# One more Strassen pair in the second block of each branch of the merge, and other blocks' forms of activations

## The chip, the core and the metric

The kernel runs on one core of a Trainium2 chip. The metric is the device time of one execution in microseconds (us); lower is better. A difference of less than 0.2% of it can't be told from no change.

## What is computed

One encoder layer on 256 tokens of width 2048, in float32. Two mixers, latent attention (`y_a`) and a matrix-memory recurrence (`y_b`), read the same normed input `u`; the merge weighs their projections with gates that are projections of `u` as well. The changed part is the merge:

```python
merged = jax.nn.sigmoid(gate_a) * (y_a @ p_a) + jax.nn.sigmoid(gate_b) * (y_b @ p_b)
x = x + merged @ w_out
```

`gate_a` and `gate_b` are columns of `u @ w_in`. Each of `p_a`, `p_b` and the two gates is a product of 256 x 2048 activations with 2048 x 2048 weights, in column blocks of 512. The cross attention and the conv-GLU feed-forward layer that follow are not touched.

## The kernel before

**Precision.** A float32 product is made of three products of rounded parts: every operand x is split into `x_hi` (rounded to fp32r) and `x_lo = x - x_hi`, and hi*hi, hi*lo and lo*hi are added up in PSUM (`three`, L641 to L643). ACT makes `w_hi` of the weights, DVE makes `w_lo`.

**The weight stream.** Weights come as chunks of 128 x 1024 (512 KB) through four slots of `w_raw`, `w_hi` and `w_lo`. The SP queue asks for the chunk of a slot anew once DVE has made `w_lo` from the old one (`lo_made`); ACT may write `w_hi` of a slot once PE is done with it (`w_used`). Two chunks are a *pair*, and there is room for two pairs: step n of the loops on ACT and DVE makes the weights of pair n + 2, while PE works on pairs n and n + 1.

**The merge** is 7 blocks (`MBLOCKS`) of 8 pairs (`KPB`): blocks 0 and 1 take `y_a` with `p_a`, 2 and 3 take `y_b` with `p_b`, 4 to 6 take `u` with the gates' weights. A block makes two column blocks of 512 for both halves of 128 tokens, in four banks of PSUM. A pair is two steps of 128 along the contraction. It is done in one of two ways:

- *plain* (`merge_plain`): 8 products of 128 x 512, each by `three`, so 24 matmuls.
- *fast* (`fast_pair`): the 2 x 2 blocks of a pair (two token halves, two column blocks) are multiplied by Strassen's scheme, with 7 products, so 21 matmuls. Four of them take sums of weights, `um_sum` (made by DVE in `fast_sums`, L1887 to L1892; split by ACT into `um_hi` at L1236 and by DVE into `um_lo` at L1907), and four take sums of activations, the pair's *form* (three of the products, e5, e6 and e7, take both). The products e1, e5, e6, e7 go into four extra banks, those of the block before. The last fast pair of a block is followed by `extra_sums`: ACT copies e1 out of PSUM (L1255), then DVE adds the others up in four steps (L1916 to L1922); `merge_main` (L1957) adds all to the block's own banks when the block is done.

`MFAST = (3, 6)` says which pairs of every block are fast: 14 in all. A form belongs to one pair of activations and is shared by the blocks that read the same activations, so there are 6 forms. `merge_form_sums` (DVE, five instructions, L1934 to L1942), `merge_form_high` (ACT, L1242) and `merge_form_low` (DVE, L1947) make one. `FORM_AT` says at which step (block, pair) of the loops the form of a given number is made.

**Order.** Each engine runs its program in the written order. On ACT, step n is: the copy of e1 where pair n is the block's last fast one, then `w_hi` of pair n + 2, then a form's high part, which waits until DVE has made the form's sums. On DVE: `extra_sums` for the last fast pair, `merge_main` for the block's last pair, then the weights of pair n + 2, then the form's sums. PE starts a block only when the extra sums of the block before are read (`extras_read`) and the first chunk's `w_lo` is made (`lo_made`).

Of the kernel before, what the change touches and what calls it, by code (L numbers as in the profile page):

```python
# [37 lines left out]
BLK = 512  # L38
# [15 lines left out]
MFAST = (3, 6)  # L54
MSUMS = MBLOCKS * len(MFAST)
MFORMS = 3 * len(MFAST)
G_GB = G_MERGE + MBLOCKS * 2 * KPB
G_WOUT = G_GB + KPB
FORM_AT = {(0, 2): 1, (1, 2): 2, (2, 2): 3, (3, 2): 4, (4, 2): 5}
# [58 lines left out]
def build(nc, x, x_t, mem, mem_by_feature, positions, cols_d, mats_d, stream, out):  # L118
    ctx = ExitStack()
    with ctx:  # L120
# [148 lines left out]
        def m_form(i):  # L269
            return (nm_hi[:, i, :], nm_sum[:, i, :], nm_lo[:, i, :]) if i < 4 else (  # L270
                nu_hi[:, i - 4, :], nu_sum[:, i - 4, :], nu_lo[:, i - 4, :])

        def m_fast(n):
            b, p = n // KPB, n % KPB
            return len(MFAST) * b + MFAST.index(p) if b < MBLOCKS and p in MFAST else None

# [112 lines left out]
        def _(pe):  # L389
# [303 lines left out]
            def merge_fast(b, p):  # L693

                i = len(MFAST) * (b // 2 if b < 4 else 2) + MFAST.index(p)
                hi, raw, lo = m_form(i)
                fast_pair(G_MERGE + 2 * (KPB * b + p), m_fast(KPB * b + p), i,
                          lambda k, rows: tuple(m_acts[b][:, 2 * p + k, half, rows] for half in range(2)),
                          lambda part: (hi[:, part], lo[:, part]), lambda m: (um_hi[:, m, :], um_lo[:, m, :]),
                          lambda c: m_bank(b, c), lambda c: m_bank(b + 1, c), p == MFAST[0], p == MFAST[-1])  # L700

            for b in range(MBLOCKS):
                for p in range(KPB):
                    if p == 0 and b:
                        pe.wait_ge(sem("extras_read"), 5 * b)
                    if p == 0 and b == 2:
                        pe.wait_ge(sem("yb_lo"), 4 * NBLK)
                    if p == 1 and b == MBLOCKS - 1:
                        pe.wait_ge(sem("mg_parts"), b)
                        merged_T(0)  # L710
                    if p == MFAST[0] and b:
                        pe.wait_ge(sem("mg_parts"), b)
                    if p == MFAST[0] and b == MBLOCKS - 1:
                        pe.wait_ge(sem("mg_lo"), 2)
                    if p in MFAST:
                        merge_fast(b, p)
                    else:
                        merge_plain(b, p)
# [187 lines left out]
        def _(act):  # L906
# [344 lines left out]
            for n in range(MBLOCKS * KPB):  # L1251
                b, p = n // KPB, n % KPB
                if p == MFAST[-1]:
                    act.wait_ge(sem("fast_done"), len(MFAST) * (b + 1))
                    act.activation(um_sum[:, 0, :], ps[:, m_bank(b + 1, 0), :], ACT.Copy).then_inc(sem("extras_read"), 1)  # L1255
                if m_fast(n + 2) is not None:
# [4 lines left out]
                if n == 0:  # L1261
                    merge_form_high(0)
# [213 lines left out]
        def _(dve):  # L1476
# [448 lines left out]
            def merge_form_sums(i):  # L1925

                q = MFAST[i % 2]
                act_t = (y_a, y_b, u)[i // 2]
# [3 lines left out]
                if i == 4:  # L1932
# [356 lines left out]
def lay_out(i):  # L2289
# [134 lines left out]
```

## Time and profile before

| | us |
|---|---|
| median of 3 runs | 1724.99 |
| lowest and highest | 1724.23, 1725.16 |
| the profiled execution's own time | 1725.04 |
| its span, from the first to the last instruction | 1723.3 |
| PE busy | 1717.2 |
| DVE busy | 1306.4 |
| ACT busy | 987.8 |

Matmuls overlap in the pipeline, so the time that one takes is longer than the distance from its start to the next one's start; what a stretch of matmuls costs is read from starts. Where a row of the timeline stands for several instructions (x2), its time runs from the first one's start to the last one's end. A time in brackets at a row's end is how long the engine stood idle ahead of it, and for whom. Block 0 of the merge begins at 488.14 us.

### The profile page before, as it was taken

To read this page: it belongs to the slowest core of one execution; us is meant where nothing else is said; L and a number is where in the kernel's file an instruction comes from. 1 tells how busy PE (TensorE), PEld (TensorE's weight loads), DVE (VectorE), ACT (ScalarE), POOL (GpSimd) and SP (SyncE) were. 2 spreads that over 40 slices of the span, in tenths; PEclk is the share of its full clock that TensorE was granted. 3 is DMA by queue.
4 is the path that set the end of the run, shared out by engine and by line. 5 is a ranking of instruction groups with operands and counts; after the bars stand their busy time and mean duration, and the time that the engine had idled before them with its cause. 6 is when DMAs were issued, how large, how long until landed. Compare 5 with 4: busy or idle time off the path is not lost.

```text
span 1723.3 us, 25512 instructions
## 1 busy us (share of the span) xinstructions
PE 1717.2 (100%) x8652; PEld 1459.6 (85%) x8652; DVE 1306.4 (76%) x1805; ACT 987.8 (57%) x1329; POOL 9.9 (1%) x22
## 2 busy tenths in 40 slices
PE   9999999999999999999999999999999999999999
PEld 7888888888888888888888888888888888888887
DVE  6788876667788888887665667777777777799888
ACT  7765655657854444555654565555555555566454
POOL 0000000000000000000000000000000000000000
PEclk9999999999999999999999999999999999999999
DMA  8566565554456666666755456555555555665565
GB/s 326 185 173 183 171 170 174 173 174 149 159 181 196 198 196 205 207 195 221 291 193 186 147 171 192 182 192 189 186 190 186 189 189 186 203 203 188 199 210 178
DMA packets 90970, 331.06 MB, mean 192 GB/s; under 512 B 10224, under 2 KB 10480, under 8 KB 89872
## 3 DMA queue, kind: packets, MB, share of 16 engines
q1 hardware_dynamic: 89424, 321.96, 56.8%
q0 software_dynamic: 1472, 8.12, 2.6%
q8 instruction: 46, 0.75, 0.2%
q14 instruction: 28, 0.23, 0.0%
HBM read 326.83 MB, written 2.10 MB: 191 GB/s over the span
## 4 chain that ended last, share of the span: by engine, by line
PE 99%; DMA 0%; DVE 0%; SPq 0%; ACT 0%; issue 0%
PE ps L424 22%; PE ps L427 11%; PE ps L643 10%; PE ps L642 10%; PE ps L641 10%; PE ps L405 8%; PE ps L407 8%; PE ps L406 8%; PE ps L527 1%; PE ps L528 1%; PE ps L526 1%; PE ps L571 1%; PE ps L570 1%; PE ps L740 0%; PE ps L585 0%; PE ps L578 0%
## 5 line engine op out<-in xcount | busy, mean ns | idle before, releaser
L1493 DVE TENSOR_TENSOR w_lo<-w_raw,w_hi 128x1024 fp32r<-128x1024 f32 x486 | 589.7, 1223 | 307.4 <-ACT w_hi L914 306.4
L914 ACT ACTIVATE w_hi<-w_raw 128x1024 fp32r<-128x1024 f32 x486 | 507.8, 1056 | 370.4 <-PE ps L427 150.0
L424 PE MATMUL ps<-u,w_hi 128*128 128x512 f32 x1664 | 580.8, 395 | 0.0
L427 PE MATMUL ps<-u,w_lo 128*128 128x256 f32 x1664 | 461.8, 278 | 0.0
L424 PEld LDWEIGHTS ps<-u,w_hi 128*128 128x128 f32 x1664 | 312.1, 188 | 72.1
L427 PEld LDWEIGHTS ps<-u,w_lo 128*128 128x128 f32 x1664 | 312.7, 188 | 0.2
L405 PE MATMUL ps<-w_hi,u 128*128 128x512 f32 x416 | 166.1, 399 | 1.0 <-DVE w_lo L1525 1.0
L407 PE MATMUL ps<-w_hi,u 128*128 128x512 f32 x416 | 162.4, 390 | 0.0
L406 PE MATMUL ps<-w_lo,u 128*128 128x512 f32 x416 | 162.2, 390 | 0.0
L643 PE MATMUL ps<-w_hi,h_lo 128*128 128x512 f32 x256 | 99.6, 389 | 0.0
L405 PEld LDWEIGHTS ps<-w_hi,u 128*128 128x128 f32 x416 | 78.3, 188 | 17.1 <-DVE u L1520 1.4
L407 PEld LDWEIGHTS ps<-w_hi,u 128*128 128x128 f32 x416 | 78.2, 188 | 16.8
L406 PEld LDWEIGHTS ps<-w_lo,u 128*128 128x128 f32 x416 | 78.4, 188 | 15.1
L1454 ACT ACTIVATE w_hi<-w_raw 128x1024 fp32r<-128x1024 f32 x52 | 54.6, 1054 | 30.9 <-PE ps L643 26.3
L2248 DVE TENSOR_TENSOR w_lo<-w_raw,w_hi 128x1024 fp32r<-128x1024 f32 x52 | 61.6, 1221 | 8.2 <-ACT w_hi L1454 8.2
L1231 ACT ACTIVATE w_hi<-w_raw 128x1024 fp32r<-128x1024 f32 x30 | 31.8, 1061 | 55.5 <-PE ps L643 39.6
L641 PE MATMUL ps<-w_hi,u 128*128 128x512 f32 x156 | 60.8, 390 | 0.0
L642 PE MATMUL ps<-w_lo,u 128*128 128x512 f32 x156 | 60.7, 389 | 0.0
L643 PE MATMUL ps<-w_hi,u 128*128 128x512 f32 x156 | 60.7, 389 | 0.0
L643 PEld LDWEIGHTS ps<-w_hi,h_lo 128*128 128x128 f32 x256 | 48.0, 188 | 9.9
L641 PE MATMUL ps<-w_hi,h_hi_b 128*128 128x512 f32 x138 | 53.7, 389 | 0.0
L642 PE MATMUL ps<-w_lo,h_hi_b 128*128 128x512 f32 x138 | 53.7, 389 | 0.0
(502 smaller groups left out, 2913.7 us busy)
## 6 DMA issues: line engine op xcount, KB each, us to landing
w_raw<-in_stream SPq DMA_DIRECT2D x600, 512.0 KB, 3.4
x_tok<-in_x SPq DMA_DIRECT2D x2, 1024.0 KB, 8.1
mem_raw<-in_mem_by_feature POOLq DMA_DIRECT2D x2, 1024.0 KB, 8.0
x_tok<-in_x POOLq DMA_DIRECT2D x2, 1024.0 KB, 8.9
mem_tok<-in_mem POOLq DMA_DIRECT2D x2, 1024.0 KB, 15.3
x_t<-in_x_t SPq DMA_DIRECT2D x7, 256.0 KB, 5.0
w_raw<-in_stream SPq DMA_DIRECT2D x4, 256.0 KB, 5.0
m_st<-ncm POOLq DMA_DIRECT2D x8, 128.0 KB, 6.4
```

The costliest lines, as they stand in the source:

```text
L405: pe.matmul(o, a_hi, b_hi, start=(kc == 0), stop=False)
L406: pe.matmul(o, a_hi, b_lo, start=False, stop=False)
L407: mm = pe.matmul(o, a_lo, b_hi, start=False, stop=(kc == last_kc))
L424: pe.matmul(ps[:, bank + m, :], w_hi[:, s, lo:lo + P], act[:, kc, :, :].rearrange("p h t -> p (h t)"), start=(kc == 0), stop=False)
L427: mm = pe.matmul(ps[:, bank + m, T:2 * T], w_lo[:, s, lo:lo + P], act[:, kc, 0, :], start=False, stop=(kc == KC - 1))
L641: pe.matmul(o, a_hi, b_hi, start=first, stop=False)
L642: pe.matmul(o, a_hi, b_lo, start=False, stop=False)
L643: return pe.matmul(o, a_lo, b_hi, start=False, stop=last)
L914: act.activation(w_hi[:, s, :], w_raw[:, s, :], ACT.Copy).then_inc(hi_made, 1)
L1454: act.activation(w_hi[:, s + k, :], w_raw[:, s + k, :], ACT.Copy).then_inc(hi_made, 1)
L1493: TTo(w_lo[:, s, :], w_raw[:, s, :], w_hi[:, s, :].bitcast(F32), ALU.subtract).then_inc(lo_made, 1)
L2248: TTo(w_lo[:, s + k, :], w_raw[:, s + k, :], w_hi[:, s + k, :].bitcast(F32), ALU.subtract).then_inc(lo_made, 1)
```

## The change

`MFORM` now lists for each block which pairs are fast and which form each takes. Blocks 0 and 2 have pairs 2 and 6 fast, blocks 1 and 3 pairs 2, 4 and 6, blocks 4 to 6 pairs 3 and 6 as before: 16 fast pairs in place of 14. There are 8 forms in place of 6, three for `y_a`, three for `y_b`, two for `u`. Forms 1, 2 and 3 are made in block 0 (steps 1, 2 and 5), forms 4, 5 and 6 in block 2 (steps 1, 2 and 5), form 7 in block 4; form 0 is begun ahead of block 0, as before, and is now finished ahead of the loop. Forms 3 and 6 are the first ones for the activations that follow, `y_b` and `u`. Before, the forms 1 to 5 were made in step 2 of blocks 0 to 4, one in each. On ACT its high part stands ahead of the weights of pair 2. The host's packing of the weights follows the new choice of pairs.

```diff
@@ -51,12 +51,14 @@
 G_ML = G_MLA + PAIRS * MLA_PER
 G_MERGE = G_ML + NBLK * KPB
 MBLOCKS = 7
-MFAST = (3, 6)
-MSUMS = MBLOCKS * len(MFAST)
-MFORMS = 3 * len(MFAST)
+MFORM = ({2: 0, 6: 1}, {2: 0, 4: 2, 6: 1}, {2: 3, 6: 4}, {2: 3, 4: 5, 6: 4}) + ({3: 6, 6: 7},) * 3
+MFAST = [sorted(forms) for forms in MFORM]
+MFIRST = [sum(len(at) for at in MFAST[:b]) for b in range(MBLOCKS + 1)]
+MSUMS = MFIRST[MBLOCKS]
+MFORMS = 8
 G_GB = G_MERGE + MBLOCKS * 2 * KPB
 G_WOUT = G_GB + KPB
-FORM_AT = {(0, 2): 1, (1, 2): 2, (2, 2): 3, (3, 2): 4, (4, 2): 5}
+FORM_AT = {(0, 1): 1, (0, 2): 2, (0, 5): 3, (2, 1): 4, (2, 2): 5, (2, 5): 6, (4, 2): 7}
 MG_BANK = (2, 0, 4, 0)
 G_CK = G_WOUT + (NBLK - 1) * KPB
 G_WOUTS = [G_WOUT, G_WOUT + KPB, G_WOUT + 2 * KPB, G_CK + KPB]
@@ -267,12 +269,12 @@
             return 4 * (c // 2) + 2 * (b % 2) + c % 2
 
         def m_form(i):
-            return (nm_hi[:, i, :], nm_sum[:, i, :], nm_lo[:, i, :]) if i < 4 else (
-                nu_hi[:, i - 4, :], nu_sum[:, i - 4, :], nu_lo[:, i - 4, :])
+            return (nm_hi[:, i % 4, :], nm_sum[:, i % 4, :], nm_lo[:, i % 4, :]) if i < 6 else (
+                nu_hi[:, i - 6, :], nu_sum[:, i - 6, :], nu_lo[:, i - 6, :])
 
         def m_fast(n):
             b, p = n // KPB, n % KPB
-            return len(MFAST) * b + MFAST.index(p) if b < MBLOCKS and p in MFAST else None
+            return MFIRST[b] + MFAST[b].index(p) if b < MBLOCKS and p in MFAST[b] else None
 
         def pair_slots(w, s):
             return w[:, s:s + 2, :].rearrange("p s n -> p (s n)")
@@ -692,12 +694,12 @@
 
             def merge_fast(b, p):
 
-                i = len(MFAST) * (b // 2 if b < 4 else 2) + MFAST.index(p)
+                i = MFORM[b][p]
                 hi, raw, lo = m_form(i)
                 fast_pair(G_MERGE + 2 * (KPB * b + p), m_fast(KPB * b + p), i,
                           lambda k, rows: tuple(m_acts[b][:, 2 * p + k, half, rows] for half in range(2)),
                           lambda part: (hi[:, part], lo[:, part]), lambda m: (um_hi[:, m, :], um_lo[:, m, :]),
-                          lambda c: m_bank(b, c), lambda c: m_bank(b + 1, c), p == MFAST[0], p == MFAST[-1])
+                          lambda c: m_bank(b, c), lambda c: m_bank(b + 1, c), p == MFAST[b][0], p == MFAST[b][-1])
 
             for b in range(MBLOCKS):
                 for p in range(KPB):
@@ -708,11 +710,11 @@
                     if p == 1 and b == MBLOCKS - 1:
                         pe.wait_ge(sem("mg_parts"), b)
                         merged_T(0)
-                    if p == MFAST[0] and b:
+                    if p == MFAST[b][0] and b:
                         pe.wait_ge(sem("mg_parts"), b)
-                    if p == MFAST[0] and b == MBLOCKS - 1:
+                    if p == MFAST[b][0] and b == MBLOCKS - 1:
                         pe.wait_ge(sem("mg_lo"), 2)
-                    if p in MFAST:
+                    if p in MFAST[b]:
                         merge_fast(b, p)
                     else:
                         merge_plain(b, p)
@@ -1250,16 +1252,16 @@
 
             for n in range(MBLOCKS * KPB):
                 b, p = n // KPB, n % KPB
-                if p == MFAST[-1]:
-                    act.wait_ge(sem("fast_done"), len(MFAST) * (b + 1))
+                if p == MFAST[b][-1]:
+                    act.wait_ge(sem("fast_done"), MFIRST[b + 1])
                     act.activation(um_sum[:, 0, :], ps[:, m_bank(b + 1, 0), :], ACT.Copy).then_inc(sem("extras_read"), 1)
+                if n == 0:
+                    merge_form_high(0)
                 if m_fast(n + 2) is not None:
                     fast_high(G_MERGE + 2 * (n + 2), m_fast(n + 2), um_sum, um_hi)
                 else:
                     split(Pos(G_MERGE), 2 * n)
                     split(Pos(G_MERGE), 2 * n + 1)
-                if n == 0:
-                    merge_form_high(0)
                 if (b, p) in FORM_AT:
                     merge_form_high(FORM_AT[b, p])
                 if b == MBLOCKS - 1 and p == 0:
@@ -1924,12 +1926,14 @@
 
             def merge_form_sums(i):
 
-                q = MFAST[i % 2]
-                act_t = (y_a, y_b, u)[i // 2]
+                b = (0, 0, 1, 2, 2, 3, 4, 4)[i]
+                act_t, q = m_acts[b], [p for p in MFAST[b] if MFORM[b][p] == i][0]
                 hi, dst, lo = m_form(i)
                 h1, h2 = n_raw[:, 0, :], n_raw[:, 1, :]
                 early, late = slice(0, P), slice(P, T)
-                if i == 4:
+                if i in (4, 5):
+                    dve.wait_ge(sem("fast_done"), MFIRST[2])
+                if i == 6:
                     dve.wait_ge(w_used, G_MERGE + 4 * KPB)
                 TTo(n_raw[:], act_t[:, 2 * q:2 * q + 2, 0, :].bitcast(F32), act_t[:, 2 * q:2 * q + 2, 1, :].bitcast(F32),
                     ALU.add).then_inc(sem("n_sums"), 1)
@@ -1975,28 +1979,27 @@
                         ).then_inc(sem("mg_lo"), 1)
 
             merge_form_sums(0)
+            merge_form_low(0)
             for n in range(MBLOCKS * KPB):
                 b, p = n // KPB, n % KPB
-                if p == MFAST[-1]:
+                if p == MFAST[b][-1]:
                     extra_sums(b, lambda c: m_bank(b + 1, c), um_sum)
                 if p == KPB - 1:
                     merge_main(b)
                 done = m_fast(n + 2)
                 if done is not None:
                     g = G_MERGE + 2 * (n + 2)
-                    if p + 2 == MFAST[0] and b:
+                    if p + 2 == MFAST[b][0] and b:
                         dve.wait_ge(sem("mg_parts"), b)
                     fast_sums(g, done, um_sum)
                     fast_lows(g, done, um_sum, um_hi, um_lo)
                 else:
                     split(Pos(G_MERGE), 2 * n)
                     split(Pos(G_MERGE), 2 * n + 1)
-                if n == 0:
-                    merge_form_low(0)
+                if (b, p - 1) in FORM_AT:
+                    merge_form_low(FORM_AT[b, p - 1])
                 if (b, p) in FORM_AT:
                     merge_form_sums(FORM_AT[b, p])
-                if (b, p - 1) in FORM_AT:
-                    merge_form_low(FORM_AT[b, p - 1])
                 if (b, p) == (1, 5):
                     dve.wait_ge(sem("sig_made"), TT * (NBLK + 1))
                     dve.wait_ge(sem("mg_parts"), 1)
@@ -2322,20 +2325,20 @@
         block(w_in, o0 + n * BLK)
     block(w_in, ga0)
     p_a, p_b, w_out = (np.asarray(i[n])[0] for n in ("p_a", "p_b", "w_out"))
-    def double(w, n0, v, m0):
+    def double(b, w, n0, v, m0):
 
         both = np.concatenate([w[:, n0:n0 + BLK], v[:, m0:m0 + BLK]], 1)
         for p in range(KPB):
             pair = both[2 * p * P:(2 * p + 2) * P].reshape(2, P, 1024).copy()
-            if p in MFAST:
+            if p in MFAST[b]:
                 pair[0] = np.roll(pair[0], BLK, axis=1)
             chunks.append(pair)
 
-    for w in (p_a, p_b):
-        for n in (0, 2):
-            double(w, n * BLK, w, (n + 1) * BLK)
+    for b in range(4):
+        w, n = (p_a, p_b)[b // 2], 2 * (b % 2)
+        double(b, w, n * BLK, w, (n + 1) * BLK)
     for n in range(3):
-        double(w_in, gb0 + n * BLK, w_in, ga0 + (n + 1) * BLK)
+        double(4 + n, w_in, gb0 + n * BLK, w_in, ga0 + (n + 1) * BLK)
     block(w_in, gb0 + 3 * BLK)
     for n in range(3):
         block(w_out, n * BLK)
```

DVE, block 0, from the weights of pair 4 on, which are made in step 2: `n_raw` is the raw sum of a form, `nm_sum` and `nm_lo` its sums and low part, `w_lo` the weights' low part, `um_sum<-w_raw` the first sum of weights of a fast pair (pair 6 in both). Before:

```order
L1493 TENSOR_TENSOR w_lo<-w_raw,w_hi 128x1024 x2
L1934 TENSOR_TENSOR n_raw<-y_a 128x512
L1937 TENSOR_TENSOR nm_sum<-n_raw 128x128
L1938 TENSOR_TENSOR nm_sum<-n_raw 128x128
L1940 SCALAR_TENSOR_TENSOR nm_sum<-nm_sum,n_raw 128x128
L1942 TENSOR_TENSOR nm_sum<-nm_sum,n_raw 128x128
L1493 TENSOR_TENSOR w_lo<-w_raw,w_hi 128x1024 x2
L1947 TENSOR_TENSOR nm_lo<-nm_sum,nm_hi 128x512
L1887 TENSOR_TENSOR um_sum<-w_raw 128x1024
```

The same place now, from the same weights (those of pair 4) on:

```order
L1495 TENSOR_TENSOR w_lo<-w_raw,w_hi 128x1024 x2
L1951 TENSOR_TENSOR nm_lo<-nm_sum,nm_hi 128x512
L1938 TENSOR_TENSOR n_raw<-y_a 128x512
L1941 TENSOR_TENSOR nm_sum<-n_raw 128x128
L1942 TENSOR_TENSOR nm_sum<-n_raw 128x128
L1944 SCALAR_TENSOR_TENSOR nm_sum<-nm_sum,n_raw 128x128
L1946 TENSOR_TENSOR nm_sum<-nm_sum,n_raw 128x128
L1495 TENSOR_TENSOR w_lo<-w_raw,w_hi 128x1024 x2
L1951 TENSOR_TENSOR nm_lo<-nm_sum,nm_hi 128x512
L1889 TENSOR_TENSOR um_sum<-w_raw 128x1024
```

Form 1's five sums have moved one step forward, behind the weights of pair 3; in their old place, between the weights of pair 4 and those of pair 5, stand the low part of form 1 and the sums of form 2, and one more low part stands ahead of pair 6's sums.

ACT, the end of block 0: `um_hi` is the high part of the weight sums of pair 6, the two rows behind it the weights of pair 7, and `um_sum<-ps` the copy of e1. Before:

```order
L1236 ACTIVATE um_hi<-um_sum 128x1024 [waits u_sums,fast_done]
L1236 ACTIVATE um_hi<-um_sum 128x1024 [waits u_sums]
L914 ACTIVATE w_hi<-w_raw 128x1024 [waits w_used,landed0]
L914 ACTIVATE w_hi<-w_raw 128x1024 [waits w_used,landed1]
L1255 ACTIVATE um_sum<-ps 128x512 [waits fast_done]
L914 ACTIVATE w_hi<-w_raw 128x1024 [waits w_used,landed2]
L914 ACTIVATE w_hi<-w_raw 128x1024 [waits w_used,landed3]
```

Now:

```order
L1238 ACTIVATE um_hi<-um_sum 128x1024 [waits u_sums,fast_done]
L1238 ACTIVATE um_hi<-um_sum 128x1024 [waits u_sums]
L916 ACTIVATE w_hi<-w_raw 128x1024 [waits w_used,landed0]
L916 ACTIVATE w_hi<-w_raw 128x1024 [waits w_used,landed1]
L1244 ACTIVATE nm_hi<-nm_sum 128x512 [waits n_sums]
L1257 ACTIVATE um_sum<-ps 128x512 [waits fast_done]
L916 ACTIVATE w_hi<-w_raw 128x1024 [waits w_used,landed2]
L916 ACTIVATE w_hi<-w_raw 128x1024 [waits w_used,landed3]
```

The high part of form 3, which waits for that form's sums (`n_sums`), stands in front of the copy of e1.

DVE, the end of block 0, from the low parts of pair 6's weight sums on: `um_sum<-ps` are the four extra sums. Before:

```order
L1907 TENSOR_TENSOR um_lo<-um_sum,um_hi 128x1024 x2
L1493 TENSOR_TENSOR w_lo<-w_raw,w_hi 128x1024 x2
L1916 TENSOR_TENSOR um_sum<-ps,um_sum 128x512
L1918 SCALAR_TENSOR_TENSOR um_sum<-ps,um_sum 128x512
L1920 TENSOR_TENSOR um_sum<-ps,um_sum 128x512
L1922 SCALAR_TENSOR_TENSOR um_sum<-ps,um_sum 128x512
L1493 TENSOR_TENSOR w_lo<-w_raw,w_hi 128x1024 x2
L1957 TENSOR_TENSOR pa<-ps,um_sum 128x1024 x2
```

Now:

```order
L1909 TENSOR_TENSOR um_lo<-um_sum,um_hi 128x1024 x2
L1495 TENSOR_TENSOR w_lo<-w_raw,w_hi 128x1024 x2
L1938 TENSOR_TENSOR n_raw<-y_b 128x512
L1941 TENSOR_TENSOR nm_sum<-n_raw 128x128
L1942 TENSOR_TENSOR nm_sum<-n_raw 128x128
L1944 SCALAR_TENSOR_TENSOR nm_sum<-nm_sum,n_raw 128x128
L1946 TENSOR_TENSOR nm_sum<-nm_sum,n_raw 128x128
L1918 TENSOR_TENSOR um_sum<-ps,um_sum 128x512
L1920 SCALAR_TENSOR_TENSOR um_sum<-ps,um_sum 128x512
L1922 TENSOR_TENSOR um_sum<-ps,um_sum 128x512
L1924 SCALAR_TENSOR_TENSOR um_sum<-ps,um_sum 128x512
L1495 TENSOR_TENSOR w_lo<-w_raw,w_hi 128x1024 x2
```

The sums of form 3 stand behind the weights of pair 7 and in front of the extra sums; block 2 has the same rows at its end, with form 6.

## Rows read from the trace of the kernel before

**Rows 1.** The page: busy time by engine; granted clock by slice.
```profile
PE 1717.2 (100%) x8652; PEld 1459.6 (85%) x8652; DVE 1306.4 (76%) x1805; ACT 987.8 (57%) x1329; POOL 9.9 (1%) x22
...
PEclk9999999999999999999999999999999999999999
```

**Rows 2.** Chain of waits, engine PE: line, releaser, total us, times, longest.
```profile
PE ps L439 <- DVE y_a L1513: 1.5, 1, 1.5
PE ps L405 <- DVE w_lo L1525: 1.0, 1, 1.0
```

**Rows 3.** Timeline of PE, merge: start us, us, engine, line, operation.
```profile
488.14 0.48 PE L641 MATMUL ps<-w_hi,y_a 128*128 128x512 f32 x1
...
499.13 0.39 PE L641 MATMUL ps<-w_hi,y_a 128*128 128x512 f32 x1
...
504.57 0.39 PE L641 MATMUL ps<-w_hi,y_a 128*128 128x512 f32 x1
...
509.40 0.39 PE L641 MATMUL ps<-w_hi,y_a 128*128 128x512 f32 x1
...
530.59 0.39 PE L641 MATMUL ps<-w_hi,y_a 128*128 128x512 f32 x1
...
572.92 0.39 PE L641 MATMUL ps<-w_hi,y_b 128*128 128x512 f32 x1
```

**Rows 4.** Timeline of DVE, block 0 of the merge.
```profile
491.41 0.68 DVE L1934 TENSOR_TENSOR n_raw<-y_a 128x512 f32<-128x512 f32 x1
...
492.99 0.29 DVE L1942 TENSOR_TENSOR nm_sum<-nm_sum,n_raw 128x128 f32<-128x128 f32 x1
...
510.58 2.36 DVE L1493 TENSOR_TENSOR w_lo<-w_raw,w_hi 128x1024 fp32r<-128x1024 f32 x2 [1.65 <-ACT w_hi L914]
512.86 0.69 DVE L1947 TENSOR_TENSOR nm_lo<-nm_sum,nm_hi 128x512 fp32r<-128x512 f32 x1
513.46 1.22 DVE L1887 TENSOR_TENSOR um_sum<-w_raw 128x1024 f32<-128x1024 f32 x1
...
520.18 1.22 DVE L1493 TENSOR_TENSOR w_lo<-w_raw,w_hi 128x1024 fp32r<-128x1024 f32 x1
...
525.96 0.69 DVE L1916 TENSOR_TENSOR um_sum<-ps,um_sum 128x512 f32<-128x512 f32 x1 [3.08 <-ACT um_sum L1255]
...
528.86 2.36 DVE L1493 TENSOR_TENSOR w_lo<-w_raw,w_hi 128x1024 fp32r<-128x1024 f32 x2
```

**Rows 5.** Timeline of ACT, block 0 of the merge.
```profile
491.44 1.27 ACT L1159 ACTIVATE sig<-ps,tiny 128x512 f32<-128x512 f32 x2
...
508.97 0.63 ACT L1242 ACTIVATE nm_hi<-nm_sum 128x512 fp32r<-128x512 f32 x1 [3.07 <-DVE nm_sum L1942]
509.50 1.99 ACT L914 ACTIVATE w_hi<-w_raw 128x1024 fp32r<-128x1024 f32 x2
...
525.33 0.60 ACT L1255 ACTIVATE um_sum<-ps 128x512 f32<-128x512 f32 x1 [3.71 <-PE ps L643]
```

**Rows 6.** Timeline of DVE, start of block 2.
```profile
571.27 2.36 DVE L1493 TENSOR_TENSOR w_lo<-w_raw,w_hi 128x1024 fp32r<-128x1024 f32 x2
...
575.81 3.49 DVE L1493 TENSOR_TENSOR w_lo<-w_raw,w_hi 128x1024 fp32r<-128x1024 f32 x3
...
582.76 1.23 DVE L1887 TENSOR_TENSOR um_sum<-w_raw 128x1024 f32<-128x1024 f32 x1 [1.82 <-DMA w_raw<-in_stream]
```

**Rows 7.** Tile w_raw, 488 to 660 us: issue to landing.
```profile
DMA to landing us min/median/max: 3.1/4.2/5.4
```

**Rows 8.** Timelines of PE and DVE, start of the program.
```profile
1.47 4.63 PE L439 MATMUL ps<-y_a 128*128 128x512 f32 x10 [1.47 <-DVE y_a L1513]
...
6.72 0.40 PE L407 MATMUL ps<-w_hi,u 128*128 128x512 f32 x1
...
8.83 0.47 PE L405 MATMUL ps<-w_hi,u 128*128 128x512 f32 x1 [1.02 <-DVE w_lo L1525]
...
7.99 0.69 DVE L1525 TENSOR_TENSOR w_lo<-w_raw,w_hi 128x512 fp32r<-128x512 f32 x1
```

## The prediction

> **What bounds the kernel now.** I read the page first: PE is busy for 1717.2 us of a span of 1723.3 us, and its granted clock is at full speed in every slice [rows 1]. So only two things can move the time: fewer matmuls, or PE standing idle. Second, PE's own waits: two, both in the program's first 9 us, 2.5 us in all [rows 2, 8]. In the merge PE never waits. The reader should see in it that a microsecond saved on ACT or DVE is worth nothing, and that one added there is free only as long as each chunk is ready when PE comes for it. The busy totals (DVE 1306.4 us) don't tell how near that is; the timelines do.
>
> **What a fast pair saves.** Pair 2 of block 0 is plain and runs from 499.13 to 504.57 us, 5.44 us for 24 matmuls. Pair 3 is fast and runs from 504.57 to 509.40, 4.83 us for 21 [rows 3]. A pair made fast gives 0.61 us; two give 1.22 us, 0.07% of the time. That is all that the change can win: the loads, the stores and everything behind the merge stay as they are.
>
> **What it adds.** Two fast pairs on ACT and DVE, and two forms, all in blocks 0 to 3, and new places for the rest. A fast pair takes DVE from 513.46 to 520.18, 6.72 us, against 2.28 us for a plain pair's two `w_lo` (510.58 to 512.86) [rows 4]. A form takes 1.87 us for its five sums (491.41 to 492.99, and the last one's 0.29) and 0.60 us for its low part (512.86 to 513.46). Behind the sums there is a third cost that no busy time shows. ACT, whose next job is the form's high part, stands still until the sums are done (3.07 us at 508.97), makes the high part (0.53 us, to 509.50), and only then the `w_hi` for which DVE's next step waits: DVE stands idle for 1.65 us at 510.58 [rows 4, 5]. So a form costs DVE 1.87 + 1.65 + 0.60 = 4.12 us where both engines are in step like this.
>
> **Block 0, by DVE's clock.** Block 0 keeps two fast pairs, so PE's work in it is unchanged: from 488.14 to 530.59 us [rows 3]. DVE's work grows from one form to three (the last for block 2), and the first fast pair moves from 3 to 2.
> - Form 0's sums end at 492.99 + 0.29 = 493.28. ACT is free (its sigmoids end at 491.44 + 1.27 = 492.71 [rows 5]) and makes the high part, 0.63 us; DVE's low part of 0.60 us ends at about 494.6. There pair 2's sums of weights begin.
> - Then, in the program's new order: pair 2 (fast) 6.72; weights of pair 3 2.28; form 1's sums 1.87 and the wait 1.65; pair 4 2.28; low part 0.60; form 2's sums 1.87 and the wait 1.65; pair 5 2.28; low part 0.60; pair 6 (fast) 6.72; pair 7 2.28; form 3's sums 1.87. That is 32.67 us, so 527.3.
> - The copy of e1 stands on ACT behind form 3's high part, which waits for these sums: 0.05 for the handing over, 0.53 for the high part, 0.63 from the start of the copy to DVE's first extra sum (525.33 to 525.96 [rows 4, 5]). Then four extra sums, 2.90 (525.96 to 528.86), and block 1's first `w_lo`, 1.22: 5.33 us. It is done at 532.6.
>
> Before, that `w_lo` was done at 528.86 + 1.22 = 530.08, just in time for PE's 530.59. PE restarts about 0.15 us after a `w_lo` that it waited for (7.99 + 0.69 = 8.68, matmul at 8.83 [rows 8]): at 532.75. PE stands idle for **2.2 us** at the start of block 1. On the way PE may wait some tenths for pair 5's or pair 6's weights. That adds nothing, since the chain at the block's end is DVE's.
>
> The trap here is DVE's idle 3.08 us ahead of the extra sums [rows 4]: form 3's sums (1.87 us) look as if they fit in. They don't, since that gap has been used up by two more forms at 4.12 us each, less what the earlier start gives back; what matters is when DVE gets there.
>
> **Block 2** has the same order with forms 4, 5 and 6, so the same 38.0 us from pair 2's first sum to the next block's first `w_lo`. Only its start differs. There DVE waits for a landing: the second chunk of block 2's pair 3 was asked for when `w_lo` of the chunk before it in its slot was done, about 575.81 + 2.36 = 578.2, and DVE began at 582.76, 4.6 us later [rows 6]; the loads of that stretch take 3.1 to 5.4 us [rows 7]. Pair 2's second chunk is asked for at 571.27 + 2.36 = 573.63, 0.7 us after the block's start at 572.92; so its sums begin 0.7 + 4.6 = 5.3 us after the start (DVE itself is free at 5.2), where in block 0 they begin 6.5 us after it. 5.3 + 38.0 + 0.15 = 43.4, against 42.33 us of PE's work in the block (530.59 to 572.92 is such a block [rows 3]): idle **1.1 us** at the start of block 3.
>
> **Blocks 1 and 3** have three fast pairs and no form's sums. DVE: 3 x 6.72 + 3 x 2.28 = 27.0 us from some 6 us after the start, so it is done at 33, and PE ends pair 6 at 42.33 - 0.61 - 5.44 = 36.3. The narrow place is pair 4, whose sums may begin only when PE is done with pair 2. DVE's part for a fast pair, 6.72 us, ends with two `um_lo` that are as large as two `w_lo` (2.28), so the pair's own `w_lo` are done some 4.4 us after PE's end of pair 2 and everything after 6.8; PE comes for the first after pair 3, 5.44 us, and for the first `um_lo` nine matmuls later, 5.44 + 9 x 0.227 = 7.5 us (0.227 is 5.44 over 24). Nothing waits. Blocks 4 to 6 keep their pairs; form 7 takes form 5's place.
>
> **Sum.** -1.22 + 2.2 + 1.1 = +2.1 us. Made against the profiled execution, 1725.04 us for a span of 1723.3, this gives a span of 1725.4; that execution is 0.05 us from the median, so 1724.99 + 2.1 = **1727.1 us**. The measurement tells no change within 0.2%, 3.4 us: I forecast no measurable difference, a little to the slow side.
>
> **Rivals.**
> - *The forms are hidden* (chance 0.08). DVE is idle 3.08 us before the extra sums of each block, and 417 us of the span in all. If the three forms of a block fit into such gaps, only the saving is left: 1724.99 - 1.22 = 1723.8. Against it speaks the count above; it would take a block 0 in which DVE reaches the extra sums 2 us sooner than I add up.
> - *PE's clock falls in the pause* (0.07), the one that ends on the other side. PE would meet a pause of 2.2 us in a dense stretch, and the trace of before has none above 1.5 us. At the program's start matmuls come every 0.44 us (ten in 4.63, the last one's end counted) where 0.227 is the rule, from 1.47 to 6.72 us [rows 8]; the page's clock row doesn't show it. If a pause brought this back for as long, 5.25 us at half speed would lose some 2.5 us: 1729.6, slower by 0.27%. One such fall decides it, as 1.3 us more than my sum does. Against it: behind the pause of 1.0 us at 8.83 matmuls go on at full speed. [...]
> - *The weights land late* (0.05). Block 2's chain starts at a landing. With 5.4 us in place of 4.6 it is 0.8 us later, and in blocks 1 and 3 the raw chunks come near to ruling too, some 0.5 us each: 1728.9. To pass 0.2% it would take landings 1.4 us later than 4.6, beyond all in [rows 7]; DMA has no bytes added, so I give it little.
> - *The stalls are there, of another size* is my forecast itself (0.80). Its bounds: block 3's pause gone (landings at 3.1 leave 1.0, so only if DVE is quicker than its rows) and block 1's at 1.5 give +0.3; both larger by half give +3.7. So 1725.3 to 1728.7.
>
> **Numbers.** Of the forecast's 0.80 some 0.03 lies above 0.2%; the clock adds 0.07, late landings 0.02: slower 0.12. Faster by 0.2% would need 3.4 us where 1.22 are to be had: 0.01. The rest, 0.87, is no change. The range leaves out the hidden forms below and the fallen clock above: 1725.3 to 1729.0.
>
> **What would show it.** PE has 6 matmuls fewer, 8646. In the chain of waits for PE there are two new rows that name `w_lo`, or the extra sums, of about 2.2 and 1.1 us, at the first matmul of blocks 1 and 3, and small ones inside blocks 0 and 2. On ACT the copy of e1 in blocks 0 and 2 is released by DVE's form sums and no longer by PE. In blocks 1 and 3, 0.61 us less between starts. Wrong would be: no wait of PE above 0.5 us in the merge (then DVE's steps are shorter or overlap), or matmuls at 0.44 us behind a pause.

## The result

The changed kernel takes 1727.49 us (median of 23 runs) against 1725.03 us for the kernel before (23 runs): ratio 1.0015, 95% interval 1.0009 to 1.0021. It is 2.5 us slower, inside the 0.2% that I had called no change. One execution of each kernel in that job was far slower (2134.86 us at a mean granted clock of 0.753, the one that was profiled, and 2888.43 us), and so was one of E1 below (1740.27 us at 0.948), and where falls of the clock are counted these three are left out. The rows shown here are those of E1, a second job of the same kernel: 1727.55 us, span 1725.8 us, clock 1.0.

The page of the changed kernel, engines' busy time and granted clock:

```profile
PE 1716.6 (99%) x8646; PEld 1458.5 (85%) x8646; DVE 1318.8 (76%) x1827; ACT 993.0 (58%) x1335; POOL 9.9 (1%) x22
...
PEclk9999999999999999999999999999999999999999
```

PE has 6 matmuls fewer and is busy 0.6 us less than in [rows 1], in a span that is 2.5 us longer. Its waits:

```profile
PE ps L643 <- DVE w_lo L1495: 3.0, 2, 1.8
PE ps L441 <- DVE y_a L1515: 1.5, 1, 1.5
PE ps L407 <- DVE w_lo L1527: 1.2, 1, 1.2
```

The last two are the start of the program, as in [rows 2]. The first is new: two waits for `w_lo` (L1495 is the old L1493), 3.0 us together, the longest 1.8. The timeline of PE shows where; the list of waits counts idle time from a matmul's modelled end, so I read the cost from starts:

```profile
488.17 0.48 PE L643 MATMUL ps<-w_hi,y_a 128*128 128x512 f32 x1
...
530.50 0.39 PE L645 MATMUL ps<-w_hi,y_a 128*128 128x512 f32 x1
532.70 0.47 PE L643 MATMUL ps<-w_hi,y_a 128*128 128x512 f32 x1 [1.80 <-DVE w_lo L1495]
533.00 0.39 PE L644 MATMUL ps<-w_lo,y_a 128*128 128x512 f32 x1
...
574.56 0.39 PE L643 MATMUL ps<-w_hi,y_b 128*128 128x512 f32 x1
...
616.66 0.39 PE L645 MATMUL ps<-w_hi,y_b 128*128 128x512 f32 x1
618.21 0.47 PE L643 MATMUL ps<-w_hi,y_b 128*128 128x512 f32 x1 [1.16 <-DVE w_lo L1495]
...
660.05 0.39 PE L643 MATMUL ps<-w_hi,u 128*128 128x512 f32 x1
```

One plain matmul follows the other after 0.227 us. Here there are 2.20 us between the last one of block 0 (530.50) and the first of block 1 (532.70), and 1.55 us between those of blocks 2 and 3 (616.66, 618.21). The kernel before reached the end of block 3 at 657.59 on its timeline:

```profile
657.59 0.39 PE L641 MATMUL ps<-w_hi,u 128*128 128x512 f32 x1
```

| from first matmul to first matmul | before, us | now, us | difference |
|---|---|---|---|
| block 0, with the pause behind it | 42.45 | 44.53 | +2.08 |
| block 1 | 42.33 | 41.86 | -0.47 |
| block 2, with the pause behind it | 42.33 | 43.65 | +1.32 |
| block 3 | 42.34 | 41.84 | -0.50 |
| all four | 169.45 | 171.88 | +2.43 |

(Before: 488.14, 530.59 and 572.92 in [rows 3] and 657.59 above; blocks 2 and 3 together took 84.67, halved here.) Behind a pause the second matmul comes 0.30 us after the first (532.70, 533.00), so blocks 1 and 3 each carry 0.07 us that is the restart's; a fast pair gave 0.54 to 0.57 us. The rest of the program is as long as it was.

DVE in block 0, in the order in which the prediction added it up:

```profile
494.00 0.69 DVE L1951 TENSOR_TENSOR nm_lo<-nm_sum,nm_hi 128x512 fp32r<-128x512 f32 x1 [0.70 <-ACT nm_hi L1244]
494.61 1.22 DVE L1889 TENSOR_TENSOR um_sum<-w_raw 128x1024 f32<-128x1024 f32 x1
...
503.60 0.68 DVE L1938 TENSOR_TENSOR n_raw<-y_a 128x512 f32<-128x512 f32 x1
...
507.12 2.36 DVE L1495 TENSOR_TENSOR w_lo<-w_raw,w_hi 128x1024 fp32r<-128x1024 f32 x2 [1.65 <-ACT w_hi L916]
...
510.00 0.68 DVE L1938 TENSOR_TENSOR n_raw<-y_a 128x512 f32<-128x512 f32 x1
...
513.51 2.36 DVE L1495 TENSOR_TENSOR w_lo<-w_raw,w_hi 128x1024 fp32r<-128x1024 f32 x2 [1.65 <-ACT w_hi L916]
...
523.11 2.35 DVE L1495 TENSOR_TENSOR w_lo<-w_raw,w_hi 128x1024 fp32r<-128x1024 f32 x2
525.38 0.68 DVE L1938 TENSOR_TENSOR n_raw<-y_b 128x512 f32<-128x512 f32 x1
...
528.43 0.69 DVE L1918 TENSOR_TENSOR um_sum<-ps,um_sum 128x512 f32<-128x512 f32 x1 [1.18 <-ACT um_sum L1257]
...
531.33 2.36 DVE L1495 TENSOR_TENSOR w_lo<-w_raw,w_hi 128x1024 fp32r<-128x1024 f32 x2
```

Pair 2's sums begin at 494.61 (I had 494.6). Form sums begin at 503.60, 510.00 and 525.38, and behind the first two DVE stands idle for 1.65 us, as it did once in [rows 4]. Where the kernel before came to the extra sums at 522.9 and waited 3.08 us for the copy of e1, DVE now comes at 527.25 and is then held for another 1.18 us. The last row is block 1's first `w_lo`, done at 531.33 + 1.22 = 532.55; PE's matmul is at 532.70. ACT in the same stretch:

```profile
505.50 0.63 ACT L1244 ACTIVATE nm_hi<-nm_sum 128x512 fp32r<-128x512 f32 x1 [5.02 <-DVE nm_sum L1946]
...
511.90 0.63 ACT L1244 ACTIVATE nm_hi<-nm_sum 128x512 fp32r<-128x512 f32 x1 [3.87 <-DVE nm_sum L1946]
...
527.28 0.63 ACT L1244 ACTIVATE nm_hi<-nm_sum 128x512 fp32r<-128x512 f32 x1 [5.22 <-DVE nm_sum L1946]
527.81 0.58 ACT L1257 ACTIVATE um_sum<-ps 128x512 f32<-128x512 f32 x1
```

ACT stands idle ahead of each of the three high parts, for DVE's sums, and the copy of e1 (L1257) starts at 527.81 right behind the third. PE was done with the last fast pair at about 525.4 (in the kernel before, where the copy waits for nothing else, it began at 525.33 [rows 5], in a block that started 0.03 us earlier). So the copy is late by 2.4 us for the sake of a form that is first used in block 2.

### The profile page after: what moved, and what is told of

It reads as the page before. It is cut to its first block, busy times and chain, and to the rows that moved or that the text cites. A ratio compares the mean times of both kernels' runs of the same rounds, so it can differ in the third digit from the quotient of the medians.

```text
span 2133.0 us, 25534 instructions
## 1 busy us (share of the span) xinstructions
PE 2127.2 (100%) x8646; PEld 1600.3 (75%) x8646; DVE 1332.3 (62%) x1827; ACT 1001.4 (47%) x1335; POOL 9.9 (0%) x22
## 4 chain that ended last, share of the span: by engine, by line
PE 99%; DMA 0%; DVE 0%; SPq 0%; ACT 0%; issue 0%
PE ps L426 22%; PE ps L429 11%; PE ps L644 10%; PE ps L643 10%; PE ps L645 10%; PE ps L409 9%; PE ps L407 9%; PE ps L408 8%; PE ps L528 2%; PE ps L529 1%; PE ps L530 1%; PE ps L572 1%; PE ps L573 1%; PE ps L587 0%; PE ps L742 0%; PE ps L580 0%
## 5 line engine op out<-in xcount | busy, mean ns | idle before, releaser
L1495 DVE TENSOR_TENSOR w_lo<-w_raw,w_hi 128x1024 fp32r<-128x1024 f32 x482 | 587.9, 1224 | 584.2 <-ACT w_hi L916 583.2
L426 PE MATMUL ps<-u,w_hi 128*128 128x512 f32 x1664 | 711.3, 456 | 0.0
L429 PE MATMUL ps<-u,w_lo 128*128 128x256 f32 x1664 | 526.2, 316 | 0.0
L426 PEld LDWEIGHTS ps<-u,w_hi 128*128 128x128 f32 x1664 | 329.9, 198 | 130.5
L429 PEld LDWEIGHTS ps<-u,w_lo 128*128 128x128 f32 x1664 | 338.5, 203 | 0.5
L407 PE MATMUL ps<-w_hi,u 128*128 128x512 f32 x416 | 194.8, 468 | 0.7 <-DVE w_lo L1527 0.7
L409 PE MATMUL ps<-w_hi,u 128*128 128x512 f32 x416 | 189.6, 456 | 0.0
L408 PE MATMUL ps<-w_lo,u 128*128 128x512 f32 x416 | 189.4, 455 | 0.0
L645 PE MATMUL ps<-w_hi,h_lo 128*128 128x512 f32 x256 | 116.6, 455 | 0.0
L409 PEld LDWEIGHTS ps<-w_hi,u 128*128 128x128 f32 x416 | 83.0, 200 | 35.1
L407 PEld LDWEIGHTS ps<-w_hi,u 128*128 128x128 f32 x416 | 82.4, 198 | 34.2 <-DVE u L1522 1.2
L644 PE MATMUL ps<-w_lo,u 128*128 128x512 f32 x156 | 71.4, 458 | 0.0
L645 PE MATMUL ps<-w_hi,u 128*128 128x512 f32 x156 | 71.2, 457 | 0.0
L643 PE MATMUL ps<-w_hi,u 128*128 128x512 f32 x156 | 71.1, 456 | 0.0
L644 PE MATMUL ps<-w_lo,h_hi_b 128*128 128x512 f32 x138 | 63.2, 458 | 0.0
L643 PE MATMUL ps<-w_hi,h_hi_b 128*128 128x512 f32 x138 | 62.9, 456 | 0.0
```

Of the source, the lines that this page charges most:

```text
L407: pe.matmul(o, a_hi, b_hi, start=(kc == 0), stop=False)
L408: pe.matmul(o, a_hi, b_lo, start=False, stop=False)
L409: mm = pe.matmul(o, a_lo, b_hi, start=False, stop=(kc == last_kc))
L426: pe.matmul(ps[:, bank + m, :], w_hi[:, s, lo:lo + P], act[:, kc, :, :].rearrange("p h t -> p (h t)"), start=(kc == 0), stop=False)
L429: mm = pe.matmul(ps[:, bank + m, T:2 * T], w_lo[:, s, lo:lo + P], act[:, kc, 0, :], start=False, stop=(kc == KC - 1))
L643: pe.matmul(o, a_hi, b_hi, start=first, stop=False)
```

## The experiments

All ran beside the kernel before, whose medians were 1724.99 (E1 to E4) and 1725.08 us (E5 to E8).

**E1, the changed kernel once more**, without an edit.

> The changed kernel as it is, for a profile at full clock. My theory (ACT and DVE fall behind in blocks 0 and 2 by the forms, and the copy of e1 stands behind the last form's high part): PE waits once at the first matmul of block 1, 2.2 us, and once at that of block 3, 1.1 us; blocks 1 and 3 are 0.61 us shorter; time 1727.1 us. Rival (the third fast pair is what starves PE): waits inside blocks 1 and 3, none above 0.5 us at their start. Rival (the clock falls in the pause): matmuls 0.44 us apart behind the first pause, granted clock under 1.000 in that stretch, and a time near 1729.

1727.55 us, ratio 1.0023 (1.0009 to 1.0036). The pauses are those above, 2.08 and 1.32 us, both at a block's start; inside blocks 1 and 3 no two starts are more than 0.31 us apart. This speaks against the third pair as the cause. The profiled execution kept its clock. But of 10 executions three had a mean granted clock of 0.999 and took 1728.86 to 1729.27 us, while seven at 1.000 took 1726.86 to 1727.66. In the first job it was 5 of 22, at 1728.47 to 1729.12.

**E2, the copy of e1 ahead of the high part.**

```diff
@@ on ACT, step n
                 if p == MFAST[b][-1]:
...
+                if p == 6 and (b, 5) in FORM_AT:
+                    merge_form_high(FORM_AT[b, 5])
...
-                if (b, p) in FORM_AT:
+                if (b, p) in FORM_AT and p != 5:
                     merge_form_high(FORM_AT[b, p])
```

> On ACT the high parts of forms 3 and 6 are made behind the copy of e1 and no longer ahead of it; all else is the changed kernel. Theory: the copy is no longer in the chain, so 0.05 + 0.53 + 0.63 = 1.2 us go from each pause: block 1's is 1.0 us, block 3's is gone; time 1724.9 us. Rival (only ACT's order matters, DVE's backlog doesn't): both pauses gone, 1723.8 us. Rival (the order on ACT doesn't matter): no change, 1727.1 us.

1724.91 us, ratio 0.9999 (0.9990 to 1.0008), as the theory said to 0.1 us. That closeness is in part luck: the pauses took 2.6 us less (1.27 and 1.32), not 2.3, from a time that was 0.4 us above the forecast. DVE at the end of block 0, then PE:

```profile
525.61 0.68 DVE L1940 TENSOR_TENSOR n_raw<-y_b 128x512 f32<-128x512 f32 x1
...
527.40 0.68 DVE L1920 TENSOR_TENSOR um_sum<-ps,um_sum 128x512 f32<-128x512 f32 x1
...
530.29 2.36 DVE L1497 TENSOR_TENSOR w_lo<-w_raw,w_hi 128x1024 fp32r<-128x1024 f32 x2
```

```profile
531.66 0.47 PE L643 MATMUL ps<-w_hi,y_a 128*128 128x512 f32 x1 [0.54 <-DVE w_lo L1497]
```

The extra sums follow form 3's sums without a wait. Block 0 with its pause takes 43.26 us (488.40 to 531.66), 0.8 us more than before and 1.27 less than in E1; block 3's pause is gone. So with DVE as late as it is, ACT's order was worth some 1.3 us of each pause, and DVE's lateness alone the other 0.8 of block 0's.

**E3, forms 3 and 6 in the next block.**

```diff
-FORM_AT = {(0, 1): 1, (0, 2): 2, (0, 5): 3, (2, 1): 4, (2, 2): 5, (2, 5): 6, (4, 2): 7}
+FORM_AT = {(0, 1): 1, (0, 2): 2, (1, 3): 3, (2, 1): 4, (2, 2): 5, (3, 3): 6, (4, 2): 7}
```

> Forms 3 and 6 (the first of the following activations) are made in step 3 of blocks 1 and 3 in place of step 5 of blocks 0 and 2. Theory: DVE reaches block 0's extra sums at 525.4, before the copy of e1 is there (525.96), as in the kernel before; no pause at the start of blocks 1 and 3, and blocks 1 and 3 have room for a form. Only the saving of 1.22 us is left: 1723.8 us. Rival (the forms 1, 2, 4, 5 alone already delay DVE past the extra sums): a pause of 0.5 us or more stays, 1724.5 us or above.

1724.14 us, ratio 0.9995 (0.9986 to 1.0004). No pause behind blocks 0 and 2, as expected, but 0.3 us too much. The place is the end of block 1, where DVE also weighs a block by a gate (the first row):

```profile
566.85 1.21 DVE L2006 TENSOR_TENSOR pa<-pa,sig 128x1024 f32<-128x1024 f32 x1
568.10 0.69 DVE L1918 TENSOR_TENSOR um_sum<-ps,um_sum 128x512 f32<-128x512 f32 x1
```

It comes to the extra sums at 568.10, while ACT's copy was there at 567.55; block 1's last matmul and block 2's first are 0.39 us apart, 0.16 us more than the usual 0.227. A form's sums cost nothing only where the engine has idle time left before the next point at which another engine waits for it.

**E4, the forms without the pairs.**

```diff
-MFORM = ({2: 0, 6: 1}, {2: 0, 4: 2, 6: 1}, {2: 3, 6: 4}, {2: 3, 4: 5, 6: 4}) + ({3: 6, 6: 7},) * 3
+MFORM = ({2: 0, 6: 1}, {2: 0, 6: 1}, {2: 3, 6: 4}, {2: 3, 6: 4}) + ({3: 6, 6: 7},) * 3
...
-                act_t, q = m_acts[b], [p for p in MFAST[b] if MFORM[b][p] == i][0]
+                act_t, q = m_acts[b], ([p for p in MFAST[b] if MFORM[b][p] == i] + [4])[0]
```

The second edit makes the two unused forms from pair 4, as before.

> All forms are made when and where the changed kernel makes them, but blocks 1 and 3 have two fast pairs (2 and 6); forms 2 and 5 are made and not used. Theory: both pauses stay as they are (2.2 and 1.1 us) and the saving is gone: 1725.0 + 3.3 = 1728.3 us. Rival (the third pair makes the pauses): no pause, 1725.0 us.

1728.61 us, ratio 1.0023 (1.0014 to 1.0033). The starts across the two pauses are 2.23 and 1.47 us apart, where E1 has 2.20 and 1.55. The pauses come with the forms alone; the third pairs take 1.1 us off (1728.61 to 1727.55). Four of 10 executions had a clock of 0.999, at 1729.82 to 1730.62 us.

**E5, one form less.** The kernel before's number of pairs and forms, at the changed kernel's places.

```diff
-MFORM = ({2: 0, 6: 1}, {2: 0, 4: 2, 6: 1}, {2: 3, 6: 4}, {2: 3, 4: 5, 6: 4}) + ({3: 6, 6: 7},) * 3
+MFORM = ({2: 0, 6: 1},) * 2 + ({2: 2, 6: 3},) * 2 + ({3: 4, 6: 5},) * 3
-FORM_AT = {(0, 1): 1, (0, 2): 2, (0, 5): 3, (2, 1): 4, (2, 2): 5, (2, 5): 6, (4, 2): 7}
+FORM_AT = {(0, 1): 1, (0, 5): 2, (2, 1): 3, (2, 5): 4, (4, 2): 5}
```

The number of forms, their numbering and the waits that go by it follow.

> Two fast pairs (2 and 6) in blocks 0 to 3 and two forms for each branch; the first form of the following activations stays in step 5 of blocks 0 and 2, ahead of the copy of e1 on ACT as in the changed kernel. Theory (the pauses come from DVE's backlog, to which each form in steps 1 and 2 adds 4.1 us): with one form less DVE makes the last form's sums by 523.2 in block 0, before the last fast pair is done, so nothing holds the copy; no pause, 1725.0 us. Rival (a form whose high part stands ahead of the copy makes a pause wherever it is): 1.2 us or more at the starts of blocks 1 and 3, 1727 us.

1725.09 us against 1725.08, ratio 1.0000 (0.9991 to 1.0009). No pause, with the high part still ahead of the copy. DVE in block 0, then ACT:

```profile
513.83 1.22 DVE L1889 TENSOR_TENSOR um_sum<-w_raw 128x1024 f32<-128x1024 f32 x1 [1.62 <-issue]
...
522.83 0.68 DVE L1936 TENSOR_TENSOR n_raw<-y_b 128x512 f32<-128x512 f32 x1
...
525.88 0.69 DVE L1918 TENSOR_TENSOR um_sum<-ps,um_sum 128x512 f32<-128x512 f32 x1 [1.18 <-ACT um_sum L1257]
```

```profile
524.73 0.63 ACT L1244 ACTIVATE nm_hi<-nm_sum 128x512 fp32r<-128x512 f32 x1 [3.21 <-DVE nm_sum L1944]
525.26 0.58 ACT L1257 ACTIVATE um_sum<-ps 128x512 f32<-128x512 f32 x1
```

The high part is out of the way at 525.26. The copy starts there, 37.22 us after the block's first matmul (488.04), against 37.19 in the kernel before (525.33 and 488.14), and the extra sums start at 525.88, as early as before. The order on ACT does harm only once DVE is late; both are needed for the full pause. But the copy is on time with nothing to spare. The form's sums end at 525.88 - 1.18 = 524.70, 1.5 us later than I expected: DVE stood idle for 1.62 us ahead of pair 6's sums (513.83). The profile names no releaser there, but pair 6's second chunk was asked for when pair 4's `w_lo` were done, at 509.51, and took 4.2 us to land. So one form less gave DVE 2.55 us (527.25 to 524.70), not 4.1; the rest it spent waiting for weights.

**E6, a longer pause.**

```diff
+                for _ in range(3 if i == 3 else 0):
+                    step(TTo(n_raw[:], act_t[:, 2 * q:2 * q + 2, 0, :].bitcast(F32),
+                             act_t[:, 2 * q:2 * q + 2, 1, :].bitcast(F32), ALU.add))
                 TTo(n_raw[:], ...
```

> The first sum of form 3 in block 0 is made four times over, some 0.72 us each, so 2.2 us are added to DVE's chain; all else is the changed kernel. Theory: the pause at the start of block 1 grows by the same 2.2 us to 4.2 us, and the time to 1727.5 + 2.2 = 1729.7 us. The clock: in some executions of the kernels with a pause of 2 us the mean granted clock was 0.999 and the time some 1.6 us longer; if the pause brings that about, it happens more often here, or always (1731.3 us), and the row of the stretch behind the pause shows a granted clock under 1 and matmuls about 0.44 us apart. Rival (the clock's dips have nothing to do with the pause): as often as in the changed kernel.

1731.39 us, ratio 1.0037 (1.0023 to 1.0051). The starts across the first pause are 4.37 us apart, 2.17 more than in E1. All five executions had a clock under 1 (0.999 or 0.998). Here a profile caught it. PE behind the pause, and the windows (the third number from the right is the granted clock):

```profile
535.21 0.47 PE L643 MATMUL ps<-w_hi,y_a 128*128 128x512 f32 x1 [3.98 <-DVE w_lo L1495]
535.51 0.40 PE L644 MATMUL ps<-w_lo,y_a 128*128 128x512 f32 x1
535.74 0.43 PE L645 MATMUL ps<-w_hi,y_a 128*128 128x512 f32 x1
535.98 0.63 PE L643 MATMUL ps<-w_hi,y_a 128*128 128x512 f32 x1
536.40 0.63 PE L644 MATMUL ps<-w_lo,y_a 128*128 128x512 f32 x1
...
538.96 0.59 PE L644 MATMUL ps<-w_lo,y_a 128*128 128x512 f32 x1
539.38 0.40 PE L645 MATMUL ps<-w_hi,y_a 128*128 128x512 f32 x1
```

```profile
488.00:530.00 42.00, 42.00 (x189) 34.48 (x188) 36.58 (x54) 22.16 (x28) 0.00 (x0) 1.00 0.59 188
530.00:535.00 5.00, 1.22 (x6) 0.68 (x4) 3.93 (x6) 4.68 (x6) 0.00 (x0) 1.00 0.00 0
535.00:539.00 4.00, 3.79 (x11) 3.05 (x12) 4.00 (x6) 0.00 (x0) 0.00 (x0) 0.62 0.63 178
539.00:543.00 4.00, 4.00 (x18) 3.30 (x17) 3.97 (x5) 1.02 (x2) 0.00 (x0) 0.95 0.61 216
```

Three matmuls still follow at 0.23 to 0.30 us, then eight are 0.42 to 0.43 us apart (535.98 to 539.38), then the old pace returns. 512 columns in 0.425 us are 1.2 GHz, in 0.227 us the 2.4 GHz level; the granted clock is 0.62 in the window from 535 to 539 and 0.95 in the next, into which the last 0.4 us fall, and it is 1.00 ahead of them, the pause itself included. Eight times 0.425 - 0.227 is 1.6 us, near to the 1.7 and 1.8 us that the executions at 0.999 took longer than those at 1.000 in E1 and E4 (medians). So it is likely that the same fall, behind one of the pauses, is what some executions of the changed kernel have; none of them was profiled. With a pause twice as long it came in all five.

"TensorE: Matmul & The Clock Gate" of the Trainium skill, section "Why this matters for your kernels", says that an idle gap of more than a certain length between bursts of matmuls sends PE back to half clock. The pause here, 3.98 us idle, is longer than that, and this trace agrees, with 1.6 us for one fall. The pauses of some 2 us in E1 and E4 are shorter than that, and yet the mean clock was 0.999 in 3 of 10 and 4 of 10 executions; there the measurement decides.

**E7, high parts one step later.**

```diff
-                if (b, p) in FORM_AT:
-                    merge_form_high(FORM_AT[b, p])
+                if (b, p - 1) in FORM_AT:
+                    merge_form_high(FORM_AT[b, p - 1])
```

> Forms in the steps of the changed kernel, but ACT makes each high part one step later, behind the next step's weights (and behind the copy of e1). Theory: DVE's wait of 1.65 us for w_hi behind each form's sums is gone (two in block 0, two in block 2) and the copy isn't held; DVE is at the extra sums by 524, before the copy; no pause at the starts of blocks 1 and 3: 1723.8 us. Rival (the amount of form work in the blocks is the cause): at least block 1's pause stays, 1 us or more, 1725 us.

1723.91 us, ratio 0.9993 (0.9984 to 1.0002). No pause; the four blocks take 168.26 us (487.81 to 656.07), 1.19 less than before. DVE in block 0:

```profile
504.81 0.29 DVE L1946 TENSOR_TENSOR nm_sum<-nm_sum,n_raw 128x128 f32<-128x128 f32 x1
505.02 2.35 DVE L1495 TENSOR_TENSOR w_lo<-w_raw,w_hi 128x1024 fp32r<-128x1024 f32 x2
...
509.47 0.29 DVE L1946 TENSOR_TENSOR nm_sum<-nm_sum,n_raw 128x128 f32<-128x128 f32 x1
509.68 2.35 DVE L1495 TENSOR_TENSOR w_lo<-w_raw,w_hi 128x1024 fp32r<-128x1024 f32 x2
...
525.63 0.69 DVE L1918 TENSOR_TENSOR um_sum<-ps,um_sum 128x512 f32<-128x512 f32 x1 [1.30 <-ACT um_sum L1257]
```

Behind both forms' sums the next `w_lo` follows at once, for ACT has made its `w_hi` while DVE was summing. The same number of forms in the same steps costs PE nothing when ACT isn't made to wait for them first. This edit does two things at once, it takes away DVE's waits and it puts the copy of e1 ahead of form 3's high part; E2 has the second alone and keeps 0.8 us of block 0's pause, so the first is worth at least that.

**E8, forms 3 and 6 in step 1 of blocks 1 and 3.**

```diff
-FORM_AT = {(0, 1): 1, (0, 2): 2, (0, 5): 3, (2, 1): 4, (2, 2): 5, (2, 5): 6, (4, 2): 7}
+FORM_AT = {(0, 1): 1, (0, 2): 2, (1, 1): 3, (2, 1): 4, (2, 2): 5, (3, 1): 6, (4, 2): 7}
```

> Forms 3 and 6 in step 1 of blocks 1 and 3, where DVE stands idle for 1.8 us until PE is done with the first fast pair; in the run that made them in step 3 DVE came 0.55 us late to block 1's extra sums and PE lost 0.2 us at the start of block 2. Theory: no pause at all, 0.2 us better than that run: 1723.9 us. Rival (step 1 delays the weight sums of pair 4, which PE then waits for): waits inside blocks 1 and 3, 1724.3 us or more.

1724.00 us, ratio 0.9994 (0.9985 to 1.0003), and no pause. DVE in block 1:

```profile
544.85 0.69 DVE L1938 TENSOR_TENSOR n_raw<-y_b 128x512 f32<-128x512 f32 x1
...
546.63 1.22 DVE L1889 TENSOR_TENSOR um_sum<-w_raw 128x1024 f32<-128x1024 f32 x1
```

The form's sums fill the time in which DVE had to wait for the first fast pair (1.82 us in E3), and pair 4's sums follow them without a gap. E3's small loss is gone (168.37 us for the four blocks, 168.66 in E3). E7 and E8 are both some 1.1 us better than the kernel before. The interval of each comparison takes in 1, so it rests on the starts: 168.26 us for the four blocks in E7 and 168.37 in E8, against 169.45. All 22 times of E7 and E8 (1723.34 to 1724.56) also lie below all 27 of the kernel before (1724.65 and more). Which of the two is better is not shown.

## Why the prediction was right

The time (1727.1 forecast, 1727.5 measured), the sign and the cause came out as forecast. The terms add up to +2.4 us measured (-0.97, +2.08, +1.32) where I had +2.1. They are off by +0.25, -0.12 and +0.22 us, so the sum is not right by large errors that cancel. By the terms of the sum:

- **Two fast pairs, -1.22 us.** -0.47 and -0.50 in blocks 1 and 3, -1.1 without the two restarts, and -1.08 to -1.19 in E8 and E7. Right in size, some 0.1 us too much; the restart behind a pause, 0.07 us each, I had left out.
- **The chain of DVE in block 0, a pause of 2.2 us.** 2.08. The start of pair 2's sums (494.6), of form 3's (525.4) and the end of block 1's first `w_lo` (532.6 forecast, 532.55 measured) were met to 0.1 us. E2, E5 and E7 take away one link each and give what the sum gives without it: 1724.9, 1725.0 and 1723.8 us forecast, 1724.91, 1725.09 and 1723.91 measured (in E2 in part by luck, and in E5 with 1.5 us of the margin that I expected gone, as said there).
- **The same chain in block 2, a pause of 1.1 us.** 1.32. DVE at the places that matter:

```profile
572.91 2.36 DVE L1495 TENSOR_TENSOR w_lo<-w_raw,w_hi 128x1024 fp32r<-128x1024 f32 x2
...
580.11 1.22 DVE L1889 TENSOR_TENSOR um_sum<-w_raw 128x1024 f32<-128x1024 f32 x1 [0.31 <-DMA w_raw<-in_stream]
...
616.84 2.36 DVE L1495 TENSOR_TENSOR w_lo<-w_raw,w_hi 128x1024 fp32r<-128x1024 f32 x2
```

  It did wait for the landing, and began pair 2's sums 580.11 - 574.56 = 5.55 us after the block's start where I had added 5.3. The chain from there to the end of the `w_lo` is 616.84 + 1.22 - 580.11 = 37.95 us, against 38.0. The term was short by the start, not by the chain. The chunk was asked for when the first row above was done, at 572.91 + 2.36 = 575.27, 0.71 us after the block's start, as forecast (0.7). From there to the sums it took 4.84 us where I had 4.6: this load took 4.5 us from issue to landing, the one in the kernel before from which I had the 4.6 took 4.2.
- **Nothing inside blocks 1 and 3.** Right; E4 shows that the third pair has no part in the pauses. The small waits that I expected inside blocks 0 and 2 aren't there either: the largest distance of two starts in them is 0.25 us.
- **The rival of hidden forms** (0.08) has fallen with E1 and E4. I had said for it that DVE is idle 3.08 us ahead of the extra sums of each block; that is so in blocks 0 and 2 of the kernel before, but in block 1 it is 2.02 us and in block 3 2.83. **The rival of the clock** (0.07) was half right: the mean granted clock was under 1 in 8 of 32 executions of the changed kernel, and such an execution takes some 1.6 us more, where I had 2.5. As they are a minority, they move the median by only 0.2 us (1727.49 with them, 1727.28 without). I had given no thought to a mechanism that acts in some executions only. **Late landings** (0.05) did not occur, apart from the 0.25 us above: in E1 the loads of the merge took 3.0 to 4.6 us.

## What to carry to other kernels

A saving on the busiest engine is worth its matmuls only if the engines that feed it keep their places: here 1.1 us saved on PE came with two chains through DVE and ACT that cost 3.4 us, though DVE was idle for 24% of the time and ACT for 42%. Read the chain from one place where an engine must wait for another to the next, and count waits between the helpers as work: a form cost DVE 2.5 us of instructions and 1.65 us of standing still, because ACT's next job was the one that waited for it. To hand work between two in-order engines, let the second take it up one step later (E7) or place it where the first was going to wait anyway (E8).

## What the runs showed beyond that

The granted clock of PE goes with the length of the pause. With a pause of 2 us in a dense stretch of matmuls its mean was under 1 in 12 of 42 executions (the first job, E1 and E4), with one of 4 us in 5 of 5 (E6), and with one of 0.7 us (E2) in none of 11. It was 1.000 in all 44 executions of E3, E5, E7 and E8 and in all 59 of the kernel before that ran beside E1 to E8. The one profile that caught the fall is E6's: it comes three matmuls behind the pause, lasts eight matmuls and costs 1.6 us. Where it comes in the executions with a pause of 2 us, no profile shows; they took 1.6 to 1.8 us more. It widens the spread of the times and moves the median by 0.2 us.

And the wait at the program's start (`w_lo` L1527) was 1.2 us in E1, 0.8 in E2, 0.5 in E4 and none in E3; block 0 of the merge began anywhere from 487.59 (E4) to 488.50 us (E6) though no experiment's edit stands ahead of it. So differences of some 0.5 us between single spans say nothing about the change.
